# Scan stage of an S5 layer: GpSimd writes the diagonals of the level matrices, VectorE both terms of its tables

## What is computed

```python
u = (h @ w_in).astype(f32)
uc = u.reshape(bsz, n_chunks, SSM_CHUNK, SSM_GROUPS, SSM_GROUP)   # 64 groups of 16 channels, 64 complex states each
def chunk_step(carry, u_blk):
    bu_re = jnp.einsum('btgk,gpk->btgp', u_blk, bb_re)            # and bu_im
    A_re, A_im, S_re, S_im = lax.associative_scan(_complex_affine_combine, (a_re, a_im, bu_re, bu_im), axis=1)
    st_re = S_re + A_re * h_re[:, None] - A_im * h_im[:, None]    # and st_im
    y = (jnp.einsum('btgp,gkp->btgk', st_re, cr) - jnp.einsum('btgp,gkp->btgk', st_im, ci))
y = jax.nn.gelu(y + d_skip * u)
```

## Time and profile before

| | us |
|---|---|
| median of 3 runs (6740.71 to 6746.28) | 6745.67 |
| the profiled execution's own time | 6745.35 |
| its span in the trace | 6743.7 |
| TensorE busy | 6211.3 (92%) |
| VectorE busy | 3288.6 (49%) |
| ScalarE busy | 2079.3 (31%) |
| GpSimd busy | 1780.9 (26%) |

### The profile page before, as it was taken

How to read it: one execution, slowest core, us unless ns; L and a number is a source line. 1 busy time by engine, 2 the same in 40 slices (tenths; PEclk the granted TensorE clock), 3 DMA queues, 4 the chain that set the end, 5 groups by cost and what they waited for, 6 DMA issues and landing times. The chain is left out here.

```text
span 6743.7 us, 88368 instructions
## 1 busy us (share of the span) xinstructions
PE 6211.3 (92%) x29650; PEld 5103.2 (76%) x29651; DVE 3288.6 (49%) x4595; ACT 2079.3 (31%) x3420; POOL 1780.9 (26%) x1556
## 2 busy tenths in 40 slices
PE   7978888999959999999979999997995999999993
PEld 5866666888848888888868888886774788888883
DVE  5546763443365545555534322224446554556554
ACT  2225552222214433444435200001111343344434
POOL 6772224880022222222210000000001222222222
PEclk9989998999979999999989999998997999999997
DMA  4443334442225766767645444333432565677766
GB/s 153 136 135 94 96 109 172 148 143 89 81 104 181 230 176 184 220 197 220 196 124 195 183 150 172 144 142 124 134 128 97 175 195 160 206 212 243 211 206 243
DMA packets 520522, 1096.72 MB, mean 163 GB/s; under 512 B 38973, under 2 KB 116893, under 8 KB 520425
## 3 DMA queue, kind: packets, MB, share of 16 engines
q1 hardware_dynamic: 408576, 805.06, 34.5%
q0 software_dynamic: 77680, 273.07, 15.9%
q10 hardware_dynamic: 34170, 17.36, 0.9%
HBM read 833.08 MB, written 261.78 MB: 162 GB/s over the span
## 5 line engine op out<-in xcount | busy, mean ns | idle before, releaser
L133 PE MATMUL conv_p<-conv_x_lo,conv_w_hi 128*128 128x512 f32 x1536 | 601.1, 391 | 0.0
L134 PE MATMUL conv_p<-conv_x_hi,conv_w_lo 128*128 128x512 f32 x1536 | 598.6, 390 | 0.0
L135 PE MATMUL conv_p<-conv_x_hi,conv_w_hi 128*128 128x512 f32 x1536 | 598.4, 390 | 0.0
L1820 DVE SCALAR_TENSOR_TENSOR m_o<-m_pO,m_weight_of,m_gate 128x512 f32<-128x512 f32 x320 | 236.8, 747 | 729.6 <-PE m_pO L1540 410.3
L1787 DVE TENSOR_TENSOR m_w_lo<-m_w_raw,m_w_hi 128x1024 fp32r<-128x1024 f32 x496 | 577.6, 1214 | 0.0
L1595 ACT ACTIVATE m_xT_hi<-m_pX 128x512 fp32r<-128x512 f32 x320 | 191.5, 599 | 1151.9 <-PE m_pB L135 994.2
L133 PE MATMUL m_pA<-m_w_lo,m_xT_hi 128*128 128x512 f32 x1280 | 517.2, 404 | 6.0 <-DVE m_xT_lo L1798 6.0
L1536 PE MATMUL m_pO<-m_w_lo,m_hT_hi 128*128 128x512 f32 x1280 | 512.8, 401 | 0.5 <-ACT m_hT_hi L1600 0.5
L1583 ACT ACTIVATE m_w_hi<-m_w_raw 128x1024 fp32r<-128x1024 f32 x512 | 505.3, 1053 | 0.0
L135 PE MATMUL m_pA<-m_w_hi,m_xT_hi 128*128 128x512 f32 x1280 | 502.8, 393 | 0.0
L134 PE MATMUL m_pA<-m_w_hi,m_xT_lo 128*128 128x512 f32 x1280 | 500.0, 391 | 0.0
(11 more groups left out here) (391 smaller groups left out, 12686.8 us busy)
## 6 DMA issues: line engine op xcount, KB each, us to landing
m_w_raw<-in_moe_w_dram SPq DMA_DIRECT2D x384, 1024.0 KB, 7.1
conv_x_hi<-hT_hi SPq DMA_DIRECT2D x24, 2048.0 KB, 8.5
conv_x_lo<-hT_lo SPq DMA_DIRECT2D x24, 2048.0 KB, 13.2
glu_ada<-in_ada_w_dram POOLq DMA_DIRECT2D x96, 256.0 KB, 3.2
a_x<-in_x_dram SPq DMA_DIRECT2D x32, 512.0 KB, 3.6
a_ada<-in_ada_w_dram POOLq DMA_DIRECT2D x64, 256.0 KB, 3.1
u<-a_stage POOLq DMA_DIRECT2D x8, 2048.0 KB, 14.2
s_u<-u SPq DMA_DIRECT2D x64, 256.0 KB, 2.6
```

The source lines that it names most:

```text
L133: pe.matmul(out, lh, rl, start=start, stop=False)
L134: pe.matmul(out, ll, rh, start=False, stop=False)
L135: return pe.matmul(out, lh, rh, start=False, stop=stop)
L1820: dve.scalar_tensor_tensor(out=ob[:, n, :], in0=pO[:, n, :], scalar=wslot[:, bass.ds(tile_, 1)], in1=gate2[:, n, :], op0=ALU.mult, op1=ALU ...
```

## The change

GpSimd no longer makes `t2p` and `t2o`. It makes the diagonals instead: one product of the identity with `tab.ha`, both broadcast, for all seven matrices of a group (128x896 elements), four of them one after the other for each block. For the first two blocks they wait for nothing, for each later one until the scan of the block two before has ended. ScalarE's seven instructions per group go. VectorE makes `t2p` and `t2o` itself, as the second step of a pattern table and the first of an output table; that one stands ahead of the wait for `carry`. The waits between VectorE and GpSimd for the terms go, and VectorE's wait for the diagonals is for one increment per group instead of seven.

```diff
--- before.py
+++ after.py
@@ -729,23 +729,20 @@
-            with pool.Fori(0, NB // 2) as i:
+            def body(i, first, last):
                 for s in range(2):
+                    b = 2 * i + s
+                    if not first:
+                        pool.wait_ge(level, LEVELS * b - LEVELS + 1)
                     for g in range(BG):
-                        q, gs, r = g % 2, bass.ds(number(i, s, g), 1), turn(i, s, g)
-                        ai = tab.pi[:, gs, :].squeeze(1)
-                        pool.wait_ge(terms_used[q], r + 1)
-                        pool.tensor_tensor(t2p[q][:], tab.b2[:, gs, :].broadcast_to([P, L, CH]),
-                                           tab.back_i[:, gs, :].squeeze(1).unsqueeze(2).broadcast_to([P, L, CH]), ALU.mult) \
-                            .then_inc(pool_terms[q], 1)
-                        pool.tensor_tensor(t2o[q][:], tab.c2[:, gs, :].broadcast_to([P, L + 1, CH]),
-                                           ai.unsqueeze(2).broadcast_to([P, L + 1, CH]), ALU.mult) \
-                            .then_inc(pool_terms[q], 1)
+                        n = bass.ds(number(i, s, g), 1)
+                        pool.tensor_tensor(M[s][:, g, :, :], ident[:].unsqueeze(1).broadcast_to([P, LEVELS, P]),
+                                           tab.ha[:, n, :].squeeze(1).unsqueeze(2).broadcast_to([P, LEVELS, P]), ALU.mult) \
+                            .then_inc(diags, 1)
+            pairs(pool, NB // 2, body)
@@ -757,23 +754,24 @@
                 c(dve.tensor_tensor(pt[q][:], tab.b1[:, gs, :].broadcast_to([P, L, CH]),
                                     tab.back_r[:, gs, :].squeeze(1).unsqueeze(2).broadcast_to([P, L, CH]), ALU.mult))
-                dve.wait_ge(pool_terms[q], 2 * r + 1)
+                c(dve.tensor_tensor(t2p[q][:], tab.b2[:, gs, :].broadcast_to([P, L, CH]),
+                                    tab.back_i[:, gs, :].squeeze(1).unsqueeze(2).broadcast_to([P, L, CH]), ALU.mult))
                 c(dve.tensor_tensor(pt[q][:], pt[q][:], t2p[q][:], ALU.add))
 ...
-                c = Chain(dve, ostep, 2 * n)
+                c = Chain(dve, ostep, 3 * n)
+                c(dve.tensor_tensor(t2o[q][:], tab.c2[:, gs, :].broadcast_to([P, L + 1, CH]),
+                                    tab.pi[:, gs, :].squeeze(1).unsqueeze(2).broadcast_to([P, L + 1, CH]), ALU.mult))
                 dve.wait_ge(y_psum, n + 1)
                 c(dve.tensor_tensor(O[s][g][:], tab.c1[:, gs, :].broadcast_to([P, L + 1, CH]),
                                     tab.pr[:, gs, :].squeeze(1).unsqueeze(2).broadcast_to([P, L + 1, CH]), ALU.mult))
-                dve.wait_ge(pool_terms[q], 2 * r + 2)
                 c(dve.tensor_tensor(O[s][g][:], O[s][g][:], t2o[q][:], ALU.add))
-                dve.sem_inc(terms_used[q], 1)
@@ -786,7 +784,7 @@
-                dve.wait_ge(diags, LEVELS * n + LEVELS)
+                dve.wait_ge(diags, n + 1)
@@ -832,9 +830,6 @@
-                for k in range(LEVELS):
-                    act.activation(M[s][:, g, k, :], ident[:], ACT.Copy, scale=tab.ha[:, bass.ds(n, 1), k]) \
-                       .then_inc(diags, 1)
```

More of the change, by code:

```diff
@@ L646, in ssm_scan @@
     y_view = y_dram.rearrange("(c t) (n f) -> n c t f", t=L, f=2 * BG * CH)
-    u_ld, pool_terms, terms_used = core.sem("s_u_loaded", 2), core.sem("s_pool_terms", 2), core.sem("s_terms_used", 2)
+    u_ld = core.sem("s_u_loaded", 2)
     tabs, zeroed = core.sem("s_tables", 2), core.sem("s_zeroed")
@@ L731, in _ @@
             pool.memset(pad[:], 0.0).then_inc(zeroed, 1)
-            with pool.Fori(0, NB // 2) as i:
+            def body(i, first, last):
                 for s in range(2):
+                    b = 2 * i + s
+                    if not first:
+                        pool.wait_ge(level, LEVELS * b - LEVELS + 1)
                     for g in range(BG):
-                        q, gs, r = g % 2, bass.ds(number(i, s, g), 1), turn(i, s, g)
-                        ai = tab.pi[:, gs, :].squeeze(1)
-                        pool.wait_ge(terms_used[q], r + 1)
-                        pool.tensor_tensor(t2p[q][:], tab.b2[:, gs, :].broadcast_to([P, L, CH]),
-                                           tab.back_i[:, gs, :].squeeze(1).unsqueeze(2).broadcast_to([P, L, CH]), ALU.mult) \
-                            .then_inc(pool_terms[q], 1)
-                        pool.tensor_tensor(t2o[q][:], tab.c2[:, gs, :].broadcast_to([P, L + 1, CH]),
-                                           ai.unsqueeze(2).broadcast_to([P, L + 1, CH]), ALU.mult) \
-                            .then_inc(pool_terms[q], 1)
+                        n = bass.ds(number(i, s, g), 1)
[3 more added lines that the diff above has]
+            pairs(pool, NB // 2, body)
         @block.vector
         def _(dve):
-            for q in range(2):
-                dve.sem_inc(terms_used[q], 1)
             dve.wait_ge(zeroed, BG + 2)
@@ L759, in table_p @@
                 gs = bass.ds(n, 1)
-                c = Chain(dve, vstep, 1 + BG + 2 * n)
+                c = Chain(dve, vstep, 1 + BG + 3 * n)
                 c(dve.tensor_tensor(pt[q][:], tab.b1[:, gs, :].broadcast_to([P, L, CH]),
                                     tab.back_r[:, gs, :].squeeze(1).unsqueeze(2).broadcast_to([P, L, CH]), ALU.mult))
-                dve.wait_ge(pool_terms[q], 2 * r + 1)
+                c(dve.tensor_tensor(t2p[q][:], tab.b2[:, gs, :].broadcast_to([P, L, CH]),
+                                    tab.back_i[:, gs, :].squeeze(1).unsqueeze(2).broadcast_to([P, L, CH]), ALU.mult))
                 c(dve.tensor_tensor(pt[q][:], pt[q][:], t2p[q][:], ALU.add))
```

## The result

The changed kernel takes 6763.0 us (median of 9 runs, 6761.4 to 6765.3) against 6744.1 us for the kernel before (9 runs): 1.0024 times the time, 95% interval 1.0014 to 1.0034. It is 19 us slower. The forecast was slower by 33.7, 6779 us, range 6752 to 6808. So the time is inside the range and the sign is right, but the size is a little over half of what was forecast. The mechanism is the one forecast; the question is which terms were too large.

What follows compares the result with a forecast made beforehand. TensorE's path was taken to bound the scan before, VectorE's chain with GpSimd collisions after the change. Blocks 20.5, start 9.2 and clock 4 sum to +33.7 us, giving 6779 us, range 6752 to 6808.

Steps and rivals of the forecast that it cites:

- VectorE's cycle: Scan loop: VectorE's own 29.6 us a block plus 5.3 of collisions with GpSimd makes 34.9, against 32.83 before.
- The clock's 4 us: Scan blocks: TensorE, waiting longer for pattern table 3, drops to 1.2 GHz; 0.4 us a block, +4, uncertain between 0 and 15.
- The bound moves to VectorE by collision with GpSimd: Scan loop: GpSimd's four operations take turns with VectorE's steps, 1.33 us each, 5.3 a block; TensorE follows VectorE.
- The GpSimd operation, 1.63 us: Scan: duration of one 128x896 diagonal product on GpSimd, extended from rows of 512 and 528 elements.
- The upper bound (2.24): Longest expected GpSimd diagonal product, from the sum of two full 128x512 tiles at 2.5 ns an element.
- the estimate of 1.97: GpSimd diagonal product of 896 elements by the Trainium skill's rate, 4497 ns for 2048 elements; total about 6795 us.
- The start, +9.2: First blocks of the scan phase: larger collisions with copies and tables; 8.3 + 1.3 + 0.9 - 1.3 us.
- The block, +2.05: Each whole scan block: 34.9 us instead of 32.83, ten times, +20.5 us.
- VectorE comes to output table 0 when carry is done: Output table 0 in each block: its new first step runs ahead of `carry`, so no wait there breaks VectorE's cycle.
- Rival A: Scan: VectorE absorbs the GpSimd operations at under 0.8 us each, TensorE gains, about 6731 us; chance 0.07.
- Rival B: Scan: cost per operation near 0.8 to 0.95 us, block time unchanged within 0.6, 6748 to 6759 us; chance 0.13.

Runs made afterwards that it cites:

- early_tables_gpsimd: early_tables with the diagonals on GpSimd, one operation per group, instead of on ScalarE: 6752.4 us, 33.7 us a block.
- early_tables: Against the kernel before: VectorE makes both terms, four pattern tables instead of two, new VectorE order, ScalarE's diagonals spread, GpSimd idle in the scan: 6695.0 us.
- more_on_gpsimd: Changed kernel plus a further GpSimd product of 128x448 into a spare tile behind each diagonal product, from block 2 on: 6797.8 us.
- half_on_gpsimd: Changed kernel with GpSimd writing the diagonals of groups 0 and 1 only, ScalarE those of 2 and 3: 6738.3 us.
- diagonals_on_gpsimd: Kernel before with GpSimd making the diagonals as well as the second terms, ScalarE none of the diagonals: 6773.8 us, 34.6 us a block.
- terms_on_vector: Kernel before with VectorE making both terms of its tables, ScalarE still writing the diagonals, GpSimd idle in the scan: 6751.7 us.

## Why the prediction was right in kind and too large

The step that failed is the size of VectorE's cycle: 34.9 us were forecast, 34.0 measured. The clock's 4 us, added to a block that VectorE bounds, failed too.

- **The bound moves to VectorE by collision with GpSimd: right.** early_tables_gpsimd against early_tables shows 3.9 us a block for it, more_on_gpsimd the dose upwards, half_on_gpsimd the dose downwards.
- **The GpSimd operation, 1.63 us: right**, 1.68. The row of the small broadcast product was the one to go by. The upper bound (2.24) was too long for this pattern of operands. So was the estimate of 1.97 worked out from the two-input rate of the Trainium skill (page "GPSIMD Engine Reference", section "Elementwise — side-by-side cycle accounting").
- **The start, +9.2: right in kind; that the sum came so near is in part luck.** Measured +8.8 in the first pair of profiles and 4.8 in the second, where the kernel before was slower by 2.5 there and the changed one faster by 1.6; so 6.8 in the mean. In the first pair blocks 0 and 1 gave +10.7 (forecast 9.6), block 2 -0.1 (0.9) and block 3 -1.6 (-1.3). The first part can be read in the changed kernel: the copies end at 479.68 instead of 477.28 (+2.4, forecast 2.3 to 2.6), then four steps of 2.12, 2.06, 2.06 and 1.94 us lose 5.4 (forecast 5.3), and block 0's `out_k` ends 8.1 us later (forecast 8.3):

```profile
474.78 4.90 DVE L750 COPY s_diag<-ident 16x16 f32<-16x16 f32 x3
479.72 2.12 DVE L758 TENSOR_TENSOR s_pt<-bc,pow_back 128x512 f32<-128x512 f32 x1
...
511.53 0.67 DVE L783 COPY s_k<-s_pK 128x496 f32<-128x496 f32 x1
```

- **The block, +2.05: the step that failed.** It was +1.05, ten blocks +10.5 instead of +20.5 (+9.9 in the second pair of profiles). The forecast set 29.6 + 5.3 = 34.9 against 32.83; VectorE's cycle is 33.98. TensorE's blocks, 34.1 us in the last six of the ten, scatter around it in the first four: 32.5, 34.0, 35.5 and 32.3. VectorE's own block was summed too high. From the rows of the changed kernel without collision it is 28.96: a pattern table takes 2.51 to 2.62 us (forecast 2.6), an output table 2.63 to 2.70 (2.7), and `out_k` 0.72, where I had put 1.0 by counting the last matrix operation twice. That is 0.6, and early_tables, with the same steps in another order, confirms it with 28.8. The collision came to 5.0 to 5.1 instead of 5.3: 0.2 to 0.3. Together the errors are some 2% of a sum of 35, but the forecast was the small difference of two such sums. The range for this term should have been set by the errors of both.
- **The clock, +4: the other term that failed.** It was 0. The drop happens in most blocks, as forecast: seven of the ten, where the kernel before has it in one. It does make the kernel product late, by 2.9 us summed over the ten blocks, not far from the 4. But the forecast added this to a block that VectorE bounds. VectorE does not wait for that product, so its cycle stays and TensorE catches up. Even in the block in which `carry` came so late that VectorE waited 1.40 us, its cycle was 33.8, since one GpSimd operation ran meanwhile. The term would have belonged to the other case, in which TensorE's path is the bound. There (diagonals_on_gpsimd) the drop costs some 1.3 us a block.
- **"VectorE comes to output table 0 when carry is done": not in every block.** In the first block shown above it waited 1.40 us for it at 726.91, and in one other 1.18. In the other eight it did not.
- **Rival A's threshold** was 0.8 us an operation; the measured cost is 1.25 (5 us for four). half_on_gpsimd, with the cost halved in number instead, lands where A said that the bound gives way, though its gain was only 0.7 us a block, not 1.7: at the chain through the turned table, 32.1 to 32.2, which A's sum overlooked. **Rival B** (the cycles meet, 6748 to 6759) ends 4 us under the result; the forecast lies 16 us above it.

Adding up between first profiles: start +8.8, ten blocks +10.5, the stretch from block 14 to the phase's end -5.3 by chance of the clock, together +14.0, and +2.5 in other phases, whose code is the same: +16.5 in span. Between the second profiles: +4.8, +9.9 and +0.9, together +15.6. So the scan gives some 14 to 16 us of the 19 between the medians. The other 3 to 5 are not explained; two executions of the kernel before differ by 3.7 us in the scan alone.

## What to carry to other kernels

Idle time of an engine is not free if it takes turns with a busy one. Before giving GpSimd work in SBUF, ask what VectorE does at that moment, and add the operation's whole length, less the 0.25 to 0.45 us measured here, to VectorE's chain. Where a forecast is the difference of two near-equal cycles, write down each cycle's error, and count every engine's bound, here also the chain from a buffer's release to the last table. The largest gain (49 us, early_tables) came with two things together: the collision gone, and that chain broken by two more buffers and another order. The first alone gave 6751.7 us (terms_on_vector), the second with the collision left in 6752.4 (early_tables_gpsimd), neither a gain over the kernel before. early_tables also spreads ScalarE's diagonals; the share of that was not measured.

## What the runs showed that I had not expected

- In diagonals_on_gpsimd 1.9 us of relief for TensorE on ScalarE's side turned into a longer idle time of TensorE at the next late table, and behind it came a stretch with part of its time at 1.2 GHz (granted clock 0.68 over 4.8 us), which made the block some 1.3 us longer than the tables required.
- The clock in one and the same stretch of one kernel differed between two executions (0.77 and 1.00, 30.0 and 24.7 us). A difference of 5 us between two single profiles of a 6745 us program proves nothing.
- Four GpSimd operations that land on a run of short matrix operations cost VectorE 5.7 us, more than on the longer table steps (4.9 to 5.1 in the loop, 5.4 at the start). That the table steps in the loop have gaps between them in which a GpSimd operation costs nothing would explain it; no run tests this.
